# The triangular masks of the recurrence move from VectorE to GpSimd

## The reference

```
x += W_out(sig(gA) * P_A(SSD(n)) + sig(gB) * P_B(DilatedAttn(n))),  n = RMSNorm(x)
x += PEER(RMSNorm(x))
```

```
Acs = jnp.cumsum((dt * A).reshape(b, c, Q, G, R), axis=2)
seg = jnp.exp(jnp.where(tril, Acs[:, :, :, None] - Acs[:, :, None, :], -jnp.inf))
CB = jnp.einsum('bclgn,bcsgn->bclsg', Cc, Bc)
y_diag = jnp.einsum('bclsgr,bcsgrp->bclgrp', CB[..., None] * seg, xg)
```

## Time and profile before

| what | value |
|---|---|
| time, median of 3 runs | 4462.01 us (4460.71 to 4466.38) |
| the profiled execution | 4471.37 us, span of its instructions 4469.6 us |
| granted TensorE clock, mean | 0.907 of full speed |
| PE busy | 3515.3 us, 79% of the span |
| DVE busy | 2929.9 us, 66% |
| ACT busy | 1817.2 us, 41% |
| POOL busy | 1219.8 us, 27% |
| HBM traffic | 326 GB/s over the span |

### The profile page before, as it was taken

The page is one execution under the profiler, slowest core; times in us unless marked ns, Lnnn a source line. Parts: engine busy times, 40 slices in busy tenths (PEclk is TensorE's granted clock), DMA queues, the critical chain, the costliest instruction groups (busy, mean ns, idle before and its releaser), DMA issues.

```text
span 4469.6 us, 40818 instructions
## 1 busy us (share of the span) xinstructions
PE 3515.3 (79%) x13294; PEld 2369.5 (53%) x13294; DVE 2929.9 (66%) x5647; ACT 1817.2 (41%) x4709; POOL 1219.8 (27%) x1102
## 2 busy tenths in 40 slices
PE   5989992776788896767689896776689887788877
PEld 4767872554566662655467662555457653222222
DVE  2641128888677759788677759778777768545544
ACT  2642111565434323556434422566434422333333
POOL 1000000332233323323233323232233332333332
PEclk8999996888899998888899998888899998999999
DMA  6444442988799987888799987898799996999998
GB/s 191 151 146 142 144 139 109 353 330 337 309 421 414 422 314 300 319 334 334 306 425 415 423 341 287 310 336 332 296 418 407 423 368 255 374 427 427 427 427 364
DMA packets 256986, 1452.41 MB, mean 325 GB/s; under 512 B 33921, under 2 KB 33921, under 8 KB 125701
## 3 DMA queue, kind: packets, MB, share of 16 engines
q0 software_dynamic: 169840, 1141.86, 64.1%
q1 hardware_dynamic: 86800, 307.82, 18.4%
q10 hardware_dynamic: 132, 0.12, 0.0%
HBM read 1447.18 MB, written 8.70 MB: 326 GB/s over the span
## 4 chain that ended last, share of the span: by engine, by line
PE 30%; DVE 26%; DMA 20%; ACT 14%; issue 10%; POOL 1%; DVEq 0%; ACTq 0%; POOLq 0%
DMA rows<-in_w_uv,idx 18%; PE banks L521 15%; DVE rows L1319 7%; PE sums L780 5%; DVE x L1328 4%; ACT arena L837 4%; DVE arena L1065 3%; PE banks L780 3%; PE banks L736 3%; ACT diag L970 1%; ACT L837 1%; DVE arena L1091 1%; ACT L959 1%; DMA a_rows<-arena 1%; ACT wgt L963 1%
## 5 line engine op out<-in xcount | busy, mean ns | idle before, releaser
L488 POOL DMA_INDIRECT rows<-in_w_uv,idx x1024 | 1161.0, 1134 | 2493.4 <-DVE x L1328 1165.9
L1319 DVE CUSTOM_DVE_ANT_0 rows<-rows,xn 128x1024 f32<-128x1024 f32 x1024 | 1247.1, 1222 | 583.4 <-DMA rows<-in_w_uv,idx 580.7
L521 PE MATMUL banks<-hT,ring 128*128 128x256 f32 x6656 | 1493.9, 384 | 8.9 <-DVE rstdB L1146 8.1
L521 PEld LDWEIGHTS banks<-hT,ring 128*128 128x128 f32 x6656 | 1280.7, 193 | 243.1 <-issue 61.6
L780 PE MATMUL sums<-rows,diag 128*128 128x512 f32 x1532 | 832.4, 675 | 318.5 <-ACT diag L970 300.8
L959 ACT ACTIVATE gelu<-hid 128x1 f32<-128x1 f32 x1024 | 206.9, 202 | 1753.8 <-DVE hid L1319 1751.8
L780 PEld LDWEIGHTS sums<-rows,diag 128*128 128x128 f32 x1532 | 296.9, 210 | 750.9 <-ACT diag L970 483.9
L1328 DVE SCALAR_TENSOR_TENSOR x<-rows,wgt,x 128x1024 f32<-128x1024 f32 x513 | 657.2, 1281 | 9.5 <-ACT wgt L963 9.5
L963 ACT ACTIVATE wgt<-gelu,gate 128x1 f32<-128x1 f32 x1024 | 301.7, 295 | 33.3
L780 PE MATMUL banks<-rows,diag 128*128 128x512 f32 x512 | 253.9, 618 | 62.2 <-ACT diag L970 62.2
L1065 DVE SCALAR_TENSOR_TENSOR arena<-banks,pr,arena 128x254 f32<-128x254 f32 (+1 forms) x512 | 245.5, 481 | 52.1 <-ACT arena L863 38.5
(11 more groups left out here) (157 smaller groups left out, 2805.2 us busy)
## 6 DMA issues: line engine op xcount, KB each, us to landing
ring<-in_w_ssd SPq DMA_DIRECT2D x192, 512.0 KB, 7.0
ring<-in_w_att SPq DMA_DIRECT2D x144, 512.0 KB, 8.2
ring<-in_w_mrg SPq DMA_DIRECT2D x128, 512.0 KB, 9.0
arena<-a_rows POOLq DMA_DIRECT2D x32, 1024.0 KB, 8.1
ring<-in_w_qry SPq DMA_DIRECT2D x64, 512.0 KB, 4.9
arena<-bias_tiles POOLq DMA_DIRECT2D x16, 1536.0 KB, 14.2
ring<-in_w_out SPq DMA_DIRECT2D x32, 512.0 KB, 8.2
rows<-in_w_uv,idx POOLq DMA_INDIRECT x1024, 12.1
```

The lines of the kernel that those rows point to most:

```text
L488: nc.gpsimd.indirect_dma_start(out=rows[n % NB][:, :], out_offset=None, in_=w_uv, in_offset=bass.IndirectOffsetOnAxis(ap=idx[:, t, s:s + 1 ...
L521: mm = pe.matmul(out, w[:, k * P:(k + 1) * P], rhs[:, k0 + k, :], start=start and k == 0, stop=stop and k == n - 1)
L1319: v.tensor_tensor_reduce(u, u, xn2[:, t, :], 1.0, 0.0, ALU.mult, ALU.add, hid[:, k:k + 1]).then_inc(u_done, 1)
```

## The change

`mask(g)` moves from the stream of DVE into that of POOL, with its waits and its two additions unchanged. Its place in the plan stays `place("ssd", g, 0.95)`; POOL gets these places as new ones, behind `decay_rows(g)`. On DVE nothing else changes.

```diff
                 decay_rows(0)
+                yield place("ssd", 0, 0.95)
+                mask(0)
                 for g in range(1, GROUPS):
                     yield place("ssd", g, 0.4)
                     pool.wait_ge(ex.sem, ex.at(m, 4 * g))
                     decay_rows(g)
+                    yield place("ssd", g, 0.95)
+                    mask(g)
...
+                def mask(g):
+
+                    pool.wait_ge(bc_in.sem, bc_in.at(m, 16 * (g + 1)))
+                    if g:
+                        pool.wait_ge(y_mm.sem, y_mm.at(m, g))
+                    for d, first, c in ((0, 1, C_MF), (1, 0, C_MB)):
+                        pool.tensor_tensor(Eb[:, :, first:first + 5:4, :], aBC[:, d].rearrange("p r (k c) -> p r k c", c=P),
+                                        spread(spread(cst[:, c:c + P], 1, 2), 1, RH), ALU.add).then_inc(masked.sem, 1)
...
                     yield place("ssd", g, 0.95)
                     if g:
                         after_heads(g - 1)
-                    mask(g)
```

More of the change, by code:

```diff
@@ L1071, in conv @@
                             ins.then_inc(c_ok.sem, 1)
[L1073 to L1080, removed]
                 def weigh(g):
```

## The result

The changed kernel takes 4532.86 us (median of 4 runs, 4525.17 to 4539.57) against 4464.19 us before: 1.0149 times the time before, 95% interval 1.0132 to 1.0166. That is 68.7 us slower where 35 were forecast. The profiled execution has a span of 4537.5 us, 67.9 more than before.

What follows compares the result with a forecast made beforehand. DVE's work was taken to bound the recurrence, in a loop with ACT's exponentials. Losses of 30 us in groups 1 to 7, 2 in group 0 and 2.4 in pass 0 summed to 35: 4497 us, range 4447 to 4540.

Steps and rivals of the forecast that it cites:

- the turns: POOL's adds and DVE's two-input instructions hold each other to their ends, alternating; chance 0.48, own range 4475 to 4520 us.
- A and B run as one block: Rival: POOL's two adds admit no DVE between; near 24 us a pass, 4534; chance 0.14 including an add near 3.4.
- In groups 1 to 7, DVE's time counts in 3 to 5 alone: Passes 1 to 3: removing DVE's mask wins at most 4.5 us a pass, 13.4 for three, nothing in groups 1, 2, 6, 7.
- POOL's add of 2.4 us: Each mask add on POOL was taken to last 2.4 us, twice DVE's time.
- The dot ahead of the mask: Group 1, passes 1 to 3: POOL's first add delays this dot, making the loop 1.75 us longer.
- The sum of a pass: Groups 1 to 7 of each of passes 1 to 3: 10.0 us longer a pass, 30 for three.
- Group 0 of passes 1 to 3: Adds wait for the broadcast and up to 2.6 us for dots: -0.6 to +2.0, taken as +0.7 each, 2 in all.
- Pass 0, group 0: Mask, exponentials, `weigh` and PE form one chain; adds take 4.8 instead of 2.36 us: 2.4 us lost, once.
- Pass 0, groups 1 to 7: No loss, since PE is busy and `weigh` is done well before PE asks.
- The cover named: Pass 0, groups 1 to 7: PE's work hides the slower mask; without it up to 2.4 us each, 17 in all.
- Gathers hidden: Gathers queued behind POOL's mask still land in time, just; rival of late gathers: over 4560 us, chance 0.01.
- The bound of 1.22 to 3.38 us for the add: Limits on POOL's add time: about -7 us in all at 1.22, +73 us, 4535, at 3.38.

Runs made afterwards that it cites:

- e1_wait_between: The changed kernel with POOL's second add of a group made to wait until the first is complete: 4498.17 us, ratio 1.0066 against the kernel before.
- e8_beside_taps: The changed kernel with each POOL add begun when ACT's first step of the third or fourth convolution is done, beside DVE's taps: 4474.87 us, ratio 1.0019.
- e5_no_mask: The kernel before with no mask adds on any engine, ACT's exponentials reading a constant tile instead: 4441.80 us, ratio 0.9951.
- e7_select: The changed kernel with POOL's two adds of a group replaced by four one-input selects of 512 columns: 4457.02 us, ratio 0.9985.
- e10_select_taps: The changed kernel with four selects replacing POOL's adds, begun after ACT's first steps of the third and fourth convolution, beside DVE's taps: 4449.19 us, ratio 0.9956.
- e3_one_input: The changed kernel with POOL taking a minimum of the broadcast tile and -1e30 instead of adding: 4467.12 us, ratio 1.0000 against the kernel before.
- e2_write_only: The changed kernel with POOL filling the same halves of the tile with -1e30 instead of adding: 4444.02 us, ratio 0.9957 against the kernel before.

## Why the prediction was wrong

The direction, the place and the holding were right; the turns were not, and with them one term was mis-sized, the hold of the dot. The step that failed is this one, as the prediction put it: "whoever started first holds the other to its end, and the two take turns, since POOL leaves a gap between instructions". POOL leaves none between two adds (the second starts 0.05 us ahead of the first one's end). They act as one block of 4.64 us, and the first-named rival, "A and B run as one block", priced at 4534 us, is what happened (4532.86). `e1_wait_between` puts the gap in, and the change then costs 31.6 us, where the forecast said 35. What spoke against that rival, that POOL gets in between DVE instructions, is true (`e8_beside_taps`, group 3), but does not hold the other way round for two adds in passes 1 to 3.

Point by point:
- In groups 1 to 7, DVE's time counts in 3 to 5 alone, for 13.4 us at most: shown, 13.9 us (`e5_no_mask`).
- POOL's add of 2.4 us: 2.35. DVE is let go 2.22 us behind its start, 0.13 before its end, which makes every hold about 0.2 us shorter than forecast.
- The dot ahead of the mask held by 1.75 us in group 1: 1.6 with the gap, 3.92 without. By groups, the forecast gave 1.75, 1.75, 1.06, 1.06, 1.6, 1.4, 1.4; with the gap 1.57, 1.59, 0.56, 0.74, 1.00, 1.61, 1.21. The sum of a pass, 10.0 forecast, is 8.3 with the gap and 21.2 without; 24 was the rival's. It took the hold less ACT's idle time, 3.1 us, in group 4, where 1.84 was measured; the hold less the mask, 3.9 - 2.27 = 1.6, is nearer.
- Group 0 of passes 1 to 3, 0.7 us longer each, 2 in all: the sign was wrong, 0.7 us shorter each (15.57 us from mask to `weigh` in place of 16.23). No dot came ahead of POOL's adds, which take 4.66 us together, so this is the low end of the -0.6 to +2.0 given.
- Pass 0, group 0, 2.4 us: 3.3, of which 1.0 is a transfer that landed later (the mask starts at 96.48, not 95.49), which differs from run to run, and 2.3 the adds.
- Pass 0, groups 1 to 7, nothing: shown (lengths 24.98 us before and after). The cover named held, though L1108 and L1115 there are held.
- Gathers hidden: shown for groups 1 to 7, where DVE waits for none. In group 0 a dot waits 3.4 to 4.4 us for one, beside POOL's adds, while ACT waits for the adds.
- The bound of 1.22 to 3.38 us for the add didn't matter (the terms given for 3.38 add up to 72, not 73 us); the range held the time by the rival with the block.

What stays open is why L1104 (L1108 of the changed kernel) gets in between two adds in pass 0 and no DVE instruction does in passes 1 to 3, though the dot does get in between selects (`e7_select`). It is not the kind of instruction alone (a plain one that came 0.6 to 1.0 us into the first add was held), nor for a dot the time at which it comes (0.6 to 1.8 us). A plain instruction that comes as late as in pass 0 (1.44 us) wasn't tried, nor was POOL's queue, which in pass 0 has no gathers behind the adds.

## What to carry to other kernels

Before an elementwise instruction goes from VectorE to GpSimd to relieve VectorE, count what VectorE runs beside it: its instructions with two SBUF inputs waited here for most of GpSimd's add, and two adds in a row held them 3.9 us to give back 2.27. The moves that paid here wrote only, or read one input and began with a VectorE stretch that reads PSUM (`e10_select_taps`). And look first at whether the engine to be relieved is late at all in that place: in four of groups 1 to 7 the mask cost nothing on DVE. It cost most, 5.4 us, in group 0, where DVE stood still for the mask's input with other work behind it.

## What was unexpected of the hardware

- Two GpSimd adds in a row leave VectorE no turn in passes 1 to 3; a wait for the first one's completion costs 0.13 us between starts (0.08 behind the end in place of 0.05 ahead) and saves 38.8 us over 21 groups (24.1 in place of 62.9). Selects in a row do leave it one (`e7_select`).
- The hold ends before the instruction, and at the same point whenever VectorE comes: 2.22 us of 2.35 for an add of 1024 fp32 columns, 0.89 us of 2.77 for a minimum with a scalar.
- The minimum with one input is slower than the add with two, 2.77 against 2.35 us; a fill takes 0.97 us, a select of 512 columns 0.63. These are the lines of `e3_one_input`, `e2_write_only` and `e10_select_taps`, with the median in the middle:

```profile
L456 POOL TENSOR_SCALAR arena<-arena x64: 2759/2771/3479, 92.9 to 3154.4; 128x1024 f32<-128x1024 f32 x64
...
L456 POOL MEMSET arena<- x64: 946/966/977, 93.1 to 3132.4; 128x1024 f32 x64
...
L460 POOL TENSOR_SCALAR_AFFINE_SELECT arena<-arena x128: 627/633/1615, 94.3 to 3137.1; 128x512 f32<-128x512 f32 x128
```
